# Attention of a two-layer hybrid decoder step: the gate is scaled by ScalarE and turned by VectorE and transfers, and the weight remainders change their places

## The reference, cut to what matters

```
z = x @ w_in;  q, k, v, g_attn = the first 1280 columns of z        (8 heads, 2 KV heads of 64)
q, k = rope(q), rope(k)
attn = softmax(q k^T / 8 over a window of 128, with a learned sink) @ v
attn = rmsnorm(attn) * gain * silu(g_attn)                          (512 columns)
```

## Time and profile before

| | us |
|---|---|
| median of 3 runs | 2550.71 (2549.84 to 2557.65) |
| the profiled execution | 2546.3, its span 2544.5 |
| TensorE busy | 2493.5 (98%) |
| VectorE busy | 1705.2 (67%) |
| GpSimd busy | 1172.3 (46%) |
| ScalarE busy | 1113.5 (44%) |
| the 16 DMA queues' packets, share of the span | 41.6% |

### The profile page before, as it was taken

How to read it: one execution, slowest core, us unless ns; L and a number is a source line. 1 busy time by engine, 2 the same in 40 slices (tenths; PEclk the granted TensorE clock), 3 DMA queues, 4 the chain that set the end, 5 groups by cost and what they waited for, 6 DMA issues and landing times. The chain is left out here.

```text
span 2544.5 us, 55195 instructions
## 1 busy us (share of the span) xinstructions
PE 2493.5 (98%) x20706; PEld 2044.3 (80%) x20706; DVE 1705.2 (67%) x3230; ACT 1113.5 (44%) x2542; POOL 1172.3 (46%) x1119
## 2 busy tenths in 40 slices
PE   8999989999999999999999999899999999999998
PEld 6788868888888788888888788688888887887887
DVE  5777777777676676654557777776777676866343
ACT  4455465555555510133334454555555554112322
POOL 2234315555556611496322443165555555116863
PEclk9999999999999999999999999999999999999999
DMA  5445552011110488765734555510111005877532
GB/s 182 154 172 185 187 186 70 27 43 43 44 38 25 175 288 293 273 216 172 264 123 154 186 179 178 190 35 31 43 43 51 31 33 195 313 270 257 170 135 91
DMA packets 176099, 365.44 MB, mean 144 GB/s; under 512 B 19104, under 2 KB 98464, under 8 KB 170272
## 3 DMA queue, kind: packets, MB, share of 16 engines
q1 hardware_dynamic: 175504, 363.11, 41.6%
q10 hardware_dynamic: 432, 0.08, 0.0%
HBM read 227.14 MB, written 137.89 MB: 143 GB/s over the span
## 5 line engine op out<-in xcount | busy, mean ns | idle before, releaser
L1947 PE MATMUL r_Z<-w_rec_parts,w_rec_xh 128*128 128x512 f32 x1920 | 610.3, 399 | 1.8 <-DVE r_kT L1768 0.9
L1947 PEld LDWEIGHTS r_Z<-w_rec_parts,w_rec_xh 128*128 128x128 f32 x1920 | 347.7, 188 | 71.9 <-issue 3.5
L1947 PE MATMUL r_Z<-w_rec_parts,w_rec_xl 128*128 128x512 f32 x960 | 375.7, 391 | 0.0
L124 PE MATMUL a_Z<-w_attn_high,w_attn_xh 128*128 128x512 f32 (+1 forms) x816 | 302.3, 370 | 11.6 <-DVE w_attn_low L211 9.7
L124 PE MATMUL a_Z<-w_attn_low,w_attn_xh 128*128 128x512 f32 (+1 forms) x816 | 290.6, 356 | 0.0
L124 PE MATMUL a_Z<-w_attn_high,w_attn_xl 128*128 128x512 f32 (+1 forms) x816 | 290.3, 356 | 0.0
L1649 ACT ACTIVATE r_E<-r_E 128x512 f32<-128x512 f32 x230 | 145.3, 632 | 294.6 <-DVE r_E L1805 292.1
L1540 POOL TENSOR_TENSOR r_qE<-r_qT,r_E 128x256 f32<-128x256 f32 x230 | 185.1, 805 | 190.6 <-ACT r_E L1649 115.4
L1947 PEld LDWEIGHTS r_Z<-w_rec_parts,w_rec_xl 128*128 128x128 f32 x960 | 180.2, 188 | 39.7
L1540 POOL TENSOR_TENSOR r_kE<-r_kT,r_E 128x256 f32<-128x256 f32 x230 | 201.2, 875 | 0.0
L124 PEld LDWEIGHTS a_Z<-w_attn_high,w_attn_xh 128*128 128x128 f32 x816 | 154.8, 190 | 39.9 <-issue 19.3
(11 more groups left out here) (338 smaller groups left out, 6409.3 us busy)
## 6 DMA issues: line engine op xcount, KB each, us to landing
dram_h_rows<-o_hb SPq DMA_DIRECT2D x34, 512.0 KB, 4.1
o_raw<-dram_hT SPq DMA_DIRECT2D x34, 512.0 KB, 4.3
o_hb<-dram_h_rows SPq DMA_DIRECT2D x34, 512.0 KB, 3.8
dram_y_all<-o_hb SPq DMA_DIRECT2D x34, 512.0 KB, 4.1
w_attn_xraw<-dram_xT SPq DMA_DIRECT2D x33, 512.0 KB, 5.7
w_rec_slot<-dram_w_in SPq DMA_DIRECT2D x16, 1024.0 KB, 8.2
o_mraw<-dram_mixT SPq DMA_DIRECT2D x32, 512.0 KB, 5.6
dram_hT<-o_hT SPq DMA_DIRECT2D x128, 128.0 KB, 2.6
```

The source lines that it names most:

```text
L124: mm = pe.matmul(out, a[:, c, :], b[:, c, :], start=(first and c == chunks[0] and a is xh and b is wh), stop=(last and c == chunks[-1] and ...
L1947: mm = pe.matmul(banks[what], x[:, c, :], w[:, cols[what]], start=(c == 0 and x is xh[k] and w is wh[c]), stop=(c == KC - 1 and x is xl[k]))
```

## The change

The gate of tiles 1 to 14 (`by_transfer`) is no longer scaled by VectorE and transposed by TensorE. ScalarE scales it into `u` (`scale_gate` in its own program, ahead of the exponentials). VectorE turns each 32x32 block (`turn_gate`, into `th`, the buffer of the tanh). The sync queue stores it to DRAM in four transfers whose rows put the blocks in their places (`store_gate`), and loads it back into `attn` (`load_gate_turned`). The gated product of those tiles reads it there, in SBUF. Tiles 15 and 16 keep the former way. `low_part` of the first chunk of a step moves ahead of `row_max`, that of the second behind the unfolding and ahead of the gated product, which itself moves behind the unfolding. ScalarE's second `high_part` moves ahead of the copy of v. GpSimd's `split_low` now also waits for the first `low_part` of its step. `values` waits for the mean square of the tile before in place of its gated product. In the output phase three semaphores get new names (`hT_st0`, `hT_st1`, `h_in` become `turned_st0`, `turned_st1`, `turned_in`); nothing else changes there.

```diff
+        def by_transfer(n):
+
+            return not isinstance(n, int) or 1 <= n <= NT - 3
+
...
+            def gate_home(n):
+                return dram["hT"][layer, n][:, 0:AW]
+
+            def store_gate(j, k):
+
+                n = 2 * j + k
+                sp.wait_ge(*S["turned"].at(n))
+                for i in range(4):
+                    sp.dma_start(gate_home(n).rearrange("(q r) (i x) -> i r q x", q=4, i=4)[i],
+                                 th[32 * i:32 * i + 32, :].rearrange("r (q x) -> r q x", q=4))                        .then_inc((S["turned_st0"], S["turned_st1"])[k].sem, 16)
+
+            def load_gate_turned(j, k):
+
+                n = 2 * j + k
+                sp.wait_ge(*(S["turned_st0"], S["turned_st1"])[k].at(64 * (j + k)))
+                sp.wait_ge(*S["uT_out"].at(n))
+                sp.dma_start(attn[:, :], gate_home(n)).then_inc(S["turned_in"].sem, 16)
 
...
@@ -649,14 +671,20 @@
             load_part(2)
             load_gate(0)
             load_x(2, 1)
+            store_gate(0, 1)
+            load_gate_turned(0, 1)
             for j in range(1, PAIRS - 1):
                 c = 4 * (j - 1)
                 exchange_part(c)
+                store_gate(j, 0)
+                load_gate_turned(j, 0)
                 store_mix(j - 1, 1)
                 load_x(j + 2, 0)
                 exchange_part(c + 1)
                 store_mix(j, 0)
                 exchange_part(c + 2)
+                store_gate(j, 1)
+                load_gate_turned(j, 1)
                 if j + 2 < PAIRS:
                     load_x(j + 2, 1)
                 exchange_part(c + 3)
@@ -665,6 +693,8 @@
             lead.load_x(sp, 0)
             following.load(sp, dram, layer, 6, 7)
             store_mix(PAIRS - 2, 1)
+            store_gate(PAIRS - 1, 0)
+            load_gate_turned(PAIRS - 1, 0)
             sp.wait_ge(*S["z_g"].at(NT))
             following.load(sp, dram, layer, 0, 4)
             sp.wait_ge(*lead.S["x_split"].at(1))
@@ -686,9 +716,12 @@
 
         @block.gpsimd
         def _(pool):
-            def split_low(j, k):
+            def split_low(j, k, behind=None):
                 n = 2 * j + k
                 pool.wait_ge(*S["x_high"].at(n + 1))
+                if behind is not None:
+                    pool.wait_ge(*S["w_split"].at(KC + behind + 1))
                 wait(pool, S["z_g"], n - 1)
                 pool.tensor_tensor(in_tokens(xl[k][:, :, :]), from_memory(xraw[k][:, :, :], layer),
                                    in_tokens(xh[k][:, :, :].bitcast(F32)), ALU.subtract).then_inc(S["x_split"].sem, 1)
@@ -742,17 +775,17 @@
             for j in range(1, PAIRS - 1):
                 c = 4 * (j - 1)
                 root(j - 1, 1)
-                split_low(j + 1, 0)
+                split_low(j + 1, 0, c - 2 if c > 0 else None)
                 rope_sum(j, 1)
                 combine(c)
                 combine(c + 1)
                 root(j, 0)
-                split_low(j + 1, 1)
+                split_low(j + 1, 1, c)
                 rope_sum(j + 1, 0)
                 combine(c + 2)
             j = PAIRS - 1
             root(j - 1, 1)
-            split_low(j + 1, 0)
+            split_low(j + 1, 0, PARTS - 2)
             rope_sum(j, 1)
             root(j, 0)
             lead.split_low(pool, 0)
@@ -772,6 +805,8 @@
                 n = 2 * j + k
                 act.wait_ge(*S["z_g"].at(n + 1))
                 wait(act, S["gate_done"], n)
+                if not isinstance(n, int) or n > 2:
+                    act.wait_ge(*S["turned_in"].at(16 * (n - 2)))
                 act.activation(th[:, :], Zg, ACT.Tanh, scale=0.5).then_inc(S["tanh_done"].sem, 1)
 
             def copy_v(j, k):
@@ -820,6 +855,19 @@
                                        scale=SCALE, accum_out=rowsum[:, h:h + 1])
                     heads = slice(4 * s, 4 * s + 4)
                     act.activation(sinke[:, heads], sinkd[:, heads], ACT.Exp).then_inc(S["exp_done"].sem, 1)
+            def scale_gate(j, k):
+                n = 2 * j + k
+                act.wait_ge(*S["rstd_done"].at(n + 1))
+                act.wait_ge(*S["gate_done"].at(n + 1))
+                if isinstance(n, int) and n == 1:
+                    act.wait_ge(*S["gT_ps"].at(1))
+                else:
+                    act.wait_ge(*S["turned"].at(n - 1))
+                act.activation(u[:, :].rearrange("p (i s d) -> p s i d", s=KV, d=HD),
+                               gate[k][:, :].rearrange("p (s i d) -> p s i d", s=KV, d=HD), ACT.Copy, scale=rstd[:, 0:1])\
+                    .then_inc(S["scaled"].sem, 1)
 
             def copy_attnT(j, k):
                 n = 2 * j + k
@@ -855,10 +903,10 @@
 
             def rest(j, k, c=None):
                 exps(j, k)
+                if c is not None:
+                    high_part(*c)
                 copy_v(j + k, 1 - k)
                 gate_tanh(j + k, 1 - k)
-                if c is not None:
-                    high_part(*c)
                 copy_attnT(j, k)
                 move_v(j + k, 1 - k)
 
@@ -896,18 +944,22 @@
             j = 1
             copy_qkT(j, 0)
             split_high(j + 1, 0)
+            scale_gate(j - 1, 1)
             rest(j, 0)
             with act.Fori(2, PAIRS) as j:
                 copy_qkT(j - 1, 1)
                 split_high(j, 1)
                 high_part(j - 2, 0)
+                scale_gate(j - 1, 0)
                 rest(j - 1, 1, (j - 2, 1))
                 copy_qkT(j, 0)
                 split_high(j + 1, 0)
                 high_part(j - 2, 2)
+                scale_gate(j - 1, 1)
                 rest(j, 0, (j - 2, 3))
             copy_qkT(PAIRS - 1, 1)
             lead.split_high(act, 0)
+            scale_gate(PAIRS - 1, 0)
             exps(PAIRS - 1, 1)
             following.round(act, lead.S, layer, 6)
             copy_v(PAIRS, 0)
@@ -1029,14 +1081,29 @@
                 n = 2 * j + k
                 dve.wait_ge(*S["rstd_done"].at(n + 1))
                 dve.wait_ge(*S["gate_done"].at(n + 1))
-                wait(dve, S["gT_ps"], n)
+                if n == NT - 1:
+                    dve.wait_ge(*S["gT_ps"].at(2))
                 dve.tensor_scalar(u[:, :].rearrange("p (i s d) -> p s i d", s=KV, d=HD),
                                   gate[k][:, :].rearrange("p (s i d) -> p s i d", s=KV, d=HD), rstd[:, 0:1], None,
                                   ALU.mult).then_inc(S["scaled"].sem, 1)
 
+            def turn_gate(j, k):
+                n = 2 * j + k
+                dve.wait_ge(*S["scaled"].at(n + 1))
+                dve.transpose(th[:, :].rearrange("p (q i t) -> p q i t", q=4, i=4),
+                              u[:, :].rearrange("p (i q t) -> p q i t", q=4, i=4)).then_inc(S["turned"].sem, 1)
             def gated(j, k):
                 n = 2 * j + k
-                dve.wait_ge(*S["gT_ps"].at(n + 1))
+                if by_transfer(n):
+                    dve.wait_ge(*S["turned_in"].at(16 * n))
+                    wait(dve, S["attnT_done"], n)
+                    wait(dve, (S["mix_st0"], S["mix_st1"])[k], 64 * j)
+                    dve.tensor_tensor(in_tokens(mixT[k][:, :, :]), in_tokens(attnT[:, :, :]),
+                                      attn[:, :].rearrange("p (i c t) -> p c i t", i=4, c=4), ALU.mult)                        .then_inc(S["uT_out"].sem, 1)
+                    return
+                dve.wait_ge(*S["gT_ps"].at(2 if n == NT - 2 else 3))
                 wait(dve, S["attnT_done"], n)
                 wait(dve, (S["mix_st0"], S["mix_st1"])[k], 64 * j)
                 dve.tensor_tensor(mixT[k][:, :, :].rearrange("p j t -> p (j t)"),
@@ -1114,17 +1181,17 @@
 
             def step(j, k, *chunks):
                 sum_squares(j - 1 + k, 1 - k)
-                row_max(j, k)
-                scale_gate(j - 1 + k, 1 - k)
                 for c in chunks[0:1]:
                     low_part(c, 2 * (1 - k))
+                row_max(j, k)
+                turn_gate(j - 1 + k, 1 - k)
                 divide(j, k)
                 rope(j + k, 1 - k)
-                gated(j - 1 + k, 1 - k)
                 unfold(j, k)
-                gates(j + k, 1 - k)
                 for c in chunks[1:2]:
                     low_part(c, 1 + (1 - k))
+                gated(j - 1 + k, 1 - k)
+                gates(j + k, 1 - k)
 
             step(1, 0)
             step(1, 1, 0, 1)
@@ -1237,7 +1304,10 @@
                 n = 2 * j + k
                 wait(pe, S["unfolded"], KV * n)
                 pe.wait_ge(*S["v_moved"].at(n + 1))
-                wait(pe, S["uT_out"], n)
+                if isinstance(n, int) and n in (1, NT - 1):
+                    pe.wait_ge(*S["uT_out"].at(n))
+                else:
+                    pe.wait_ge(*S["ms_done"].at(n))
                 for r in (0, 64):
                     for s in range(KV):
                         d, queries = slice(HD * s, HD * s + HD), slice(r, r + 64)
@@ -1335,7 +1405,6 @@
                 sum_squares(j - 1 + k, 1 - k)
```

(5 more changed lines are left out.)

26 lines of the change are left out of this document (13 added, 13 removed).

## The result

The changed kernel takes 2586.53 us (median of 4 runs, 2581.03 to 2592.30) against 2552.59 of the kernel before (4 runs, 2549.84 to 2557.65): 1.0123 times as long, 95% interval 1.0088 to 1.0158. The forecast was 2567 in a range of 2540 to 2588, slower with a chance of 0.58. The direction and the range held; 2567 was 19.5 too low. The profiled execution took 2581.03 (span 2579.2), against 2546.3 of before. Of the 53 executions of the kernel before that the experiments are compared with, two took 3519.65 and 5040.14 us and are left out of the ratios; the others took 2547 to 2562.

What follows compares the result with a forecast made beforehand. TensorE bounds the kernel before; after the change a step takes the longer of 18.86 and L + 12.74. Terms give +9.1 us per layer, +18.2, so 2564.5 or 2568.9 by base; predicted 2567, range 2540 to 2588.

Steps and rivals of the forecast that it cites:

- What TensorE loses: TensorE, 28 tiles: four transposes fewer save 0.44 us each, 12.3 us in all; its own step would be 18.86.
- The chain behind L: VectorE's work from the first remainder's end to the next step's begin: 12.74 us, including 0.85 for the blocked small maximum.
- L: Time from a step's begin to the first remainder's end: 6.31 us at best, later through memory, queue or combinations.
- K: Time from the first remainder's end (L) to the next step's begin, 12.74 us in the prediction's sum.
- The gate's way through memory: Gate's stores and load: gated product ends 0.8 us into the next step, delaying ScalarE by 0.65; L 6.96, step 19.70.
- rival 3: Trip through memory is long, four stores at 3.49 us: 2605, half of it 2586; chance 0.15.
- T: Time in a step at which VectorE's turn of the gate ends, forecast as L + 5.04 us.
- GpSimd's combinations: Beside the second remainder and gated product: behind four, 0.85 us more; odd steps 7 to 13 get L 7.8, 20.55.
- The sync queue in even steps: Even steps' high_part waits until 5.1 us for the previous chunk's stores, held by the queue: L 7.7, step 20.45.
- The sum: Steps 3 to 14 +11.1 us per layer, step 2 -0.44, step 15 -1.6: +9.1 per layer, +18.2.
- Rival 1: TensorE stays the bound at the values' wait for the unfolding, deciding at L = 6.1: 2533 us; chance 0.23.
- Rival 2: On VectorE, neither the small maximum nor the gated product blocks on GpSimd: constant 11.9, 2543 us; chance 0.13.

Runs made afterwards that it cites:

- combine late: Changed kernel with late split and reordered sync queue, plus GpSimd's combinations after the gated product and two mix stores behind the gate's: 2540.29 us, 0.9941 of before.
- Split late: Changed kernel with GpSimd's split_low waiting for the step's divisions in place of the first remainder: 30 us less than the changed kernel by medians, 27 by ratios.
- no combination: Changed kernel with GpSimd's combinations cut to one column, part of the gate weights left out: 15 us less than the changed kernel.
- queue's order: Changed kernel with store_mix and load_x ahead of the gate's stores and load in odd steps: 18.5 us less than it by medians, 14.5 by ratios.
- split without wait: Changed kernel with split_low's new wait removed, so it starts once its input is there: 6 us less than the changed kernel by medians, 3 by ratios.
- gate before part: Changed kernel with remainders, high_part and split_low back as before the change, and the gate's stores and load ahead of exchange_part: 70 us slower than before.
- scaling first: gate before part with scale_gate ahead of the first high_part on ScalarE: no different from gate before part.
- remainders only: Changed kernel with the gate scaled by VectorE and transposed by TensorE as before, moved remainders kept: 24 us slower than before.
- both of these: Changed kernel with the edits of Split late and queue's order together: 2550.13 us, no difference from before.
- gated first: both of these with the gated product ahead of the second remainder: slower than both of these by 37 us, 31 by ratios.
- even half's order: scaling first with the next part's load and gate weights' loads issued ahead of the gate's load in the even half: 47.5 us less by medians.

## Why the prediction came out as it did

**What TensorE loses: right, a little short.** 0.44 per step were costed, 19.30 - 18.80 = 0.50 measured, in step 2 of the changed kernel and in combine late's steps with chunks. Over 28 tiles that is 14 us for 12.3.

**The chain behind L: right in each term.** 12.74 were costed, 12.89 measured in layer 0. The small maximum took 1.07 in place of 0.16: 0.91, costed 0.85; the turn 0.70, costed 0.62. Split late takes the first away, and K falls by 0.92. This term is worth some 22 us, the largest of all; with what else the moved split frees it is 27 to 30. What the sum did not have is layer 1, whose K is 13.0 to 13.2: its rows were taken from layer 0 alone. The rule that the prediction drew from the Trainium skill (SBUF — State Buffer, "SBUF: two separate sides") would put the loser's whole wait there, and the trace agrees: L1006 ended with `split_low`.

**The gate's way through memory: failed, and rival 3 with it.** The prediction let the load land at T + 7.75 and the gated product wait for it. By the rows of step 7 the turn ends at 181.66 and the tanh, which waits for the load, starts at 187.48: 5.8. The four stores were issued in 1.79, by shape as I chose, but the load was issued 1.4 after the last issue's end, and took 2.6. Landings, median us:

```profile
dram_g_parts<-w_attn_part_high SPq DMA_DIRECT2D x28, 512.0 KB, 3.4
dram_g_parts<-w_attn_part_low SPq DMA_DIRECT2D x28, 512.0 KB, 4.6
...
dram_hT<-a_th SPq DMA_DIRECT2D x112, 64.0 KB, 1.8
a_attn<-dram_hT SPq DMA_DIRECT2D x28, 256.0 KB, 2.6
```

64 KB landed in 1.8, where I took the 2.6 of 128 KB, and the load took 2.6, its lower bound, where I took 3.75. So the wait for this load did not reach L in the changed kernel; what the trip does to the stores of the parts is told below. Step 5, where I charged the load alone, took 19.49 and not 19.70 in layer 0. In layer 1 it took 20.45, but there `high_part` waited 0.86 for the stores of the chunk before.

**GpSimd's combinations: the place was right, the size too small.** I charged 0.85 for the gated product behind four of them; against no combination, where L of the odd steps is 6.27, the changed kernel has 7.74, 1.47 more. Both instructions met them: the remainder 1.66 for 1.28, the product 1.09 to 1.76 for 0.69. That the odd steps (copy at 1.7) still came out at 20.62 to 20.65 for 20.55 is luck: the failed step above had charged 0.65 that was not there. In layer 1 they took 20.91 to 20.95. Without combinations these steps took 19.15.

**The sync queue in even steps: right in the step, wrong in the mechanism.** `high_part` was forecast at 5.1 and came at 5.25 to 5.6 in layer 0 and at 4.8 to 5.2 in layer 1, in step 4 at 6.4 and 6.1. "Its stores wait for the queue, not for it" is false: in step 7 the remainder ended at 189.37 and its stores were issued from 189.40, with the queue free before. What was longer is their landing: 4.6 for 3.8, with `store_mix`'s stores and the load of x issued just ahead of them. The queue's order matters by what is in flight beside the part stores: with those transfers moved earlier, in queue's order, the same stores to the same places landed in 3.9, and 0.8 per even step of layer 0 came back. Which of the transfers ahead slows them no run separates.

**The sum.** Steps 3 to 14 came out 14.7 and 16.2 longer in the two layers, forecast 11.1: 8.7 of the 16.5 by which the profiled execution exceeds the 2564.5 of the sum. Of these, steps 4 hold 1.3 and 1.1, the other even steps of layer 0 0.3 to 0.65 each, and in layer 1 step 5 0.75 and the odd steps from 7 on 0.4 each. Step 15 got shorter by 1.3 and 1.9, forecast 1.6. The other 7.8 are outside these steps, where I had forecast nothing: 1.2 ahead of step 2, and 6.7 between layer 0's step 16 and layer 1's step 2. Two waits of TensorE in and behind layer 0's output phase are longer there (2.2, before none of that kind; 2.0 for 1.3), and the granted clock fell twice, below. These make about 6.2 of the 6.7.

**The rivals.** Rival 1 (TensorE stays the bound) did not happen in the changed kernel: its point of decision, L = 6.1, was met by step 3 alone, with L = 6.08 (below the 6.31 that the prediction called the best), and even that step took 18.97: with K at 12.89 the point lies at 5.9. Its price was about right: combine late, in which the chain is short enough, takes 2540.29 (0.9941 of before), for 2533. Rival 2 is refuted by the small maximum at 1.07 and the gated product at 1.09 to 1.76. Rival 3's halved price, 2586, is the time measured, and its mechanism was not there: that agreement is chance.

## What to carry to other kernels

A wait of an engine is room for a moved instruction only as far as what it then runs beside stays the same: the remainder fitted nearly into VectorE's wait, but it pulled GpSimd's split along into a four-column instruction's place, and taking the split away from there gave 27 to 30 us. When work leaves the engine that bounds, look for every pair of VectorE and GpSimd instructions that now overlap, and order the pair by a wait of the one that has slack; here two such waits on GpSimd and two changes in a queue's order turned +31 us into -15 (both by the ratios). Where a load is on its way, put ahead of its reader whatever does not need it.

## What the runs showed of the hardware

**A four-column instruction waits as long as a long one.** 128x4 took 0.16 alone and 1.07 to 1.19 beside `split_low`; 128x1024 took 1.28 alone and up to 3.31. In both cases VectorE's instruction ran on to the end of the split or beyond: at 1.07 it ended with it, and at 3.31 (step 3 of split without wait) 1.08 behind it.

**The granted clock can fall behind a short wait, or not.** Windows of the changed kernel (us, then busy time of each engine, granted clock, DMA share, GB/s), and two of the kernel before around the same place:

```profile
900.00:903.00 3.00, 1.30 (x69) 1.19 (x68) 0.60 (x2) 1.41 (x5) 3.00 (x3) 0.99 0.02 5
903.00:906.00 3.00, 3.00 (x10) 2.42 (x10) 0.00 (x0) 0.60 (x1) 1.62 (x1) 0.50 0.00 0
906.00:909.00 3.00, 3.00 (x25) 2.92 (x25) 0.32 (x2) 1.20 (x8) 0.00 (x0) 0.94 0.00 0
...
1105.00:1110.00 5.00, 5.00 (x18) 3.96 (x17) 4.93 (x4) 0.72 (x2) 5.00 (x4) 0.73 0.36 91
```
```profile
880.00:890.00 10.00, 8.26 (x161) 6.45 (x160) 3.80 (x7) 5.05 (x11) 8.90 (x9) 1.00 0.07 28
890.00:900.00 10.00, 10.00 (x59) 8.52 (x58) 5.13 (x10) 1.85 (x9) 2.11 (x5) 1.00 0.37 113
```

TensorE had waited 1.7 us (`r_M` for `r_qG`) ahead of 902.3, and the clock then stood at 0.50, the lower of its two levels (1.2 GHz), for about 3.8 us; the kernel before has the same wait of 1.7, ended at 887.87, and kept 1.00. The second fall, 0.73 over 1105 to 1110, follows a wait of 2.0 that took 1.3 before. Together they cost some 3.3 us (0.50 of 3 us, and 0.07 of the 25 us from 1100, over which the clock was 0.93). In gate before part and scaling first, with steps of 22 to 28 us, the mean over the span fell to 0.984 and 0.980.

**VectorE can wait for many of GpSimd's instructions in a row.** Combine late's profiled execution makes TensorE wait once for 5.4 us in layer 0's output phase, with the clock at 0.66 over the ten microseconds from 1120 on. Its rows:

```profile
1101.77 5.04 POOL L2430 TENSOR_TENSOR o_bl<-o_tmp,o_bh 128x512 fp32r<-128x512 f32 x4
...
1104.50 11.02 DVE L2666 SCALAR_TENSOR_TENSOR o_hb<-o_th,o_hb 128x1024 f32<-128x1024 f32 x1
...
1106.78 1.41 POOL L2435 TENSOR_TENSOR o_pl<-o_praw,o_ph 128x256 fp32r<-128x256 f32 x2
...
1108.16 6.27 POOL L2424 TENSOR_TENSOR o_tmp<-o_raw 128x512 f32<-128x512 f32 x5
...
1122.12 0.79 PE L2738 MATMUL o_HT<-o_block_high,o_bh 128*128 128x512 f32 x1 [5.41 <-DVE o_s L2633]
```

One instruction of VectorE takes 11.02, where the shortest of its 34 takes 1.22. GpSimd works without a gap from before its start until 1114.43, and it ends 1.09 behind that. Eight of GpSimd's instructions start in that while, and VectorE gets in ahead of none of them. In the kernel before the same instruction started at 1110.41, as far into the same four (2.71, here 2.73), and took 3.40: there it got in behind them, and GpSimd's next two took 2.41 in place of 1.41. What decides between the two no run shows. All that VectorE does behind it is late, `o_s` included, for which TensorE waits.

**What stays open.** The same 11.0 and 5.4 stand in the traces of eight of the twelve experiments (remainders only, split late, both of these, split without wait, no combination, gated first, even half's order and combine late), and not in those of the other four, of the kernel before and of the changed kernel. Remainders only has it with the gate's former way, so it does not need the new transfers. From step 16 to layer 1's step 2 these eight take 997 to 1001 us and the other six 987 to 993 (combine late 1331.44 - 333.32 = 998.1; the kernel before 986.8, from 341.10 in the earlier trace rows and 1327.89 for layer 1's step 2). Each kernel has one trace, so whether this comes with the kernels or with single executions is not known; if with the kernels, some 10 us more are to be had.
